# First attention weights loaded behind the last rwkv projections instead of at the end of the rwkv stage

## The chip, the cores and the metric

The kernel runs on one core of one Trainium2 chip. The metric is the device time of one execution in microseconds. The core has five engines with a program each: TensorE (PE; its weight loads are shown apart as PEld), VectorE (DVE), ScalarE (ACT), GpSimd (POOL) and SyncE (SP). They share SBUF and PSUM and wait for each other with semaphores. Here SyncE only issues DMAs, which 16 DMA engines carry out. The engines' own instructions come by the same 16 DMA engines, in packets of 16 KB, which the profile lists as the queues q8 and q14 "instruction".

## The reference

One inference step of one decoder layer, for a prompt of 1024 rows and 64 sample rows (1088 rows in all), width 1024, float32. What matters here is the first half of the layer:

```python
u = _rmsnorm(h, norm_mix)
proj = u @ w_in
P = proj[..., :RWKV_PROJ]                 # r, k, v and three small parts
q, k, v = ...                             # the other columns, 3 x 512
rw_out, new_shift, new_wkv = _rwkv7(P, shift_state, wkv_state, ...)   # 8 heads x 64
att = _rmsnorm(attend(q, k, v), attn_out_norm)                        # 8 heads x 64
h = h + jnp.concatenate([rw_out, att], axis=-1) @ w_out
```

`new_shift` is the last projected row of the prompt and of each sample, and is an output. Then follow a mixture of experts, a gated embedding and a last norm, which the change doesn't touch.

## The kernel before

The program is a row of stages: token projection inputs, small inputs, rwkv, attention, output projection, routing, experts, finish. Each stage is one block; all engines meet in a barrier at its end. Between two blocks lies a small one in which GpSimd clears the semaphores of the next (`clear`, L2292), with barriers of its own. No engine starts in the attention block before SyncE has left the rwkv block.

**rwkv** (`rwkv`, L220 ff.) works on J = 4 pairs of heads, 128 columns each. All four pairs use the same tile `g.w3`, 128 partitions x 3072 floats, with one third each for the weights of r, k and v. It outlives the stage, and attention uses the same bytes for the weights of its q, k and v (1536 KB, 12 KB in each partition). The profile calls it `w`.

TensorE's program alternates `between(j)` and `inverse_and_steps(j)`. In `between(j)` the projections of pair j+1 are cut up among the work of pair j (L415). `inverse_and_steps(j)` first does the last third of v's projection of pair j, then interleaves two things: the inverses of the chunks of pair j (L620, L622, L624: small 64x64 matmuls, in runs of up to 32) and the 17 state steps of pair j-1 (L633 to L663), each of which waits for the one before through VectorE (L1080, L1084) and ScalarE (L850). For j = 0 there are no steps, for j = 4 no inverses. I call the stretch for j = 1, 2 and 3 from its first L633 to its last step **mixed stretch** 1, 2 and 3.

SyncE's program is written by hand. For each pair it waits until a projection has been evacuated, and issues in `last_rows(q, j)` two small stores of the last rows (L350: 128 rows of 4 bytes; L351: 128 rows of 32 bytes), and behind them the load of the next pair's third of `w3` (L333, 512 KB; none for the last pair). `last_rows("v", j)` comes just as mixed stretch j begins, so a 512 KB load runs beside mixed stretches 1 and 2, and none beside 3. Behind it `load_small` (L336, L338) issues four small loads beside stretch 1, none beside 2 and 3. SyncE then waits for the state (L369, semaphore `c_sev`, set by the last step) and, much later, for the stage's result (L378). At the end of its loop it issues the load of the first attention weights (L389, semaphore `qkv_in`), then waits for all the stores (L390 to L393) and goes into the barrier.

**Attention** begins on TensorE with `project(0)`: it waits for `qkv_in` (L1221), then multiplies (L1227). SyncE begins with eight loads of tables (L1184, L1185) and the first 5 MB of the key cache (L1186). GpSimd begins with two memsets (L1211, L1213).

Of the kernel before, what the change touches and what calls it, by code (L numbers as in the profile page):

```python
# [17 lines left out]
J = H // 2  # L18
# [200 lines left out]
def rwkv(nc, g):  # L219

    with ExitStack() as ctx:
# [7 lines left out]
        k, kk, r, v, tmp = (sb(n, [128, T]) for n in ("k", "kk", "r", "v", "tmp"))  # L229
# [88 lines left out]
        s = {n: sem(n) for n in names}  # L318
# [10 lines left out]
        with nc.Block() as block:  # L329
            @block.sync  # L330
            def _(sp):
                def load_w3(q, j):
                    sp.dma_start(w3[:, KIND[q], :, :], g.d_wrkv[j, KIND[q]]).then_inc(s["w3_" + q], 16)  # L333

                def load_small(j):
                    sp.dma_start(wwa[j % 2][:, :], g.d_w2a2[:, 128 * j:128 * j + 128]).then_inc(small[j % 2], 16)  # L336
                    for i in range(3):
                        sp.dma_start(edge[j % 2][:, i, :], g.d_shT[128 * j + RW * i:128 * j + RW * i + 128, :]).then_inc(small[j % 2], 16)  # L338

                def load_wg(j):  # L340
                    sp.dma_start(wg2[j % 2][:, :], g.d_g2[:, 128 * j:128 * j + 128]).then_inc(wg_in[j % 2], 16)

                def load_s0(j):
                    sp.dma_start(s0[j % 2][:, :, :].rearrange("p b v -> p (b v)"), g.d_stT[128 * j:128 * j + 128, :]).then_inc(s0_in[j % 2], 16)

                def last_rows(q, j):
                    row = 128 * j + RW * KIND[q]
                    sp.wait_ge(s[q + "_ev"], 3 * j + 3)
                    sp.wait_ge(s[q + "_ends"], j + 1)
                    sp.dma_start(g.o_pshift[row:row + 128, :], RAW[q][:, S:S + 1]).then_inc(s[q + "_outs"], 16)  # L350
                    sp.dma_start(g.o_sshift[row:row + 128, :], ends[j % 2][:, KIND[q], :]).then_inc(s[q + "_outs"], 16)  # L351
                    if j + 1 < J:
                        sp.wait_ge(s[q + "_mm"], 3 * j + 3)
                        load_w3(q, j + 1)

                load_small(0)
                load_w3("k", 0)
                load_w3("r", 0)
                load_w3("v", 0)
                load_s0(0)  # L360
                load_small(1)
                load_s0(1)
                load_wg(0)
                load_wg(1)
                for j in range(-1, J + 1):
                    jn, jp = after(j), before(j)
                    if jp is not None:
                        sp.wait_ge(s["c_sev"], (NC + 1) * (jp + 1))
                        sp.dma_start(g.o_pwkv[128 * jp:128 * jp + 128, :], st[:, NC % 2, :]).then_inc(s["c_outs"], 16)  # L369
                        sp.wait_ge(s["d_in"], jp + 1)  # L370
                        sp.dma_start(g.o_swkv[128 * jp:128 * jp + 128, :], sn[:, :, :].rearrange("p b v -> p (b v)")).then_inc(s["c_outs"], 16)
                        if jp + 2 < J:
                            load_s0(jp + 2)
                    if jn is not None:
                        last_rows("k", jn)
                    if jp is not None:
                        sp.wait_ge(s["g_ev"], 3 * jp + 3)
                        sp.dma_start(g.rw[128 * jp:128 * jp + 128, :], cen).then_inc(s["rw_out"], 16)  # L378
                        if jp + 2 < J:
                            load_wg(jp + 2)  # L380
                    if jn is not None:
                        last_rows("r", jn)
                        last_rows("v", jn)
                        if jn + 2 < J:
                            load_small(jn + 2)

                for q in "rkv":
                    sp.wait_ge(s[q + "_mm"], 3 * J)
                sp.dma_start(g.w3[:, :], g.d_wqkv[0].rearrange("p k i c -> p (k i c)")).then_inc(g.qkv_in, 16)  # L389
                for q in "rkv":  # L390
                    sp.wait_ge(s[q + "_outs"], 32 * J)
                sp.wait_ge(s["c_outs"], 32 * J)
                sp.wait_ge(s["rw_out"], 16 * J)  # L393
# [1982 lines left out]
```

## Time and profile before

| | |
|---|---|
| median of 3 runs | 1954.55 us |
| lowest and highest | 1946.48 and 1960.20 us |
| the profiled execution | 1968.97 us |
| its span, first to last instruction | 1967.0 us |
| outside the span | 1.97 us |
| TensorE busy | 1672.5 us, 85% of the span |
| mean granted TensorE clock | 0.899 |
| rwkv stage in this execution | about 103 to 738 us |
| attention stage | about 741 to 1158 us |

The profile is one execution. It took 14.4 us (0.7%) more than the median of the runs, which differ among themselves by 13.7 us. Times in it are from the start of the span. Queue rows (SPq) show when SyncE issued a DMA and for how long it was busy issuing it; "landing" is the time from issue until the data are there. A PE row's bracket is the idle time before it and what ended it.

### The profile page before, as it was taken

What the parts mean: (1) busy time and instruction counts of PE and PEld (TensorE: products, weight loads), DVE (VectorE), ACT (ScalarE), POOL (GpSimd) and SP (SyncE); (2) the same over time, 40 slices, a digit from 0 to 9 for tenths busy, and PEclk for the clock granted to TensorE, in tenths of its full rate; (3) what the DMA queues carried; (4) which work ended last, traced back from release to release, by engine and by line L of the source; (5) the groups of instructions that cost most, each with busy time, mean ns of one, the idle gap of its engine ahead of it and who ended that gap; (6) DMA issues with size and microseconds to landing.
All of it is one profiled execution on the core that took longest, in us unless ns stands there. A gap on an engine that the chain in (4) does not pass through costs nothing. (4 is left out here: it accounts for less than half of the span.)

```text
span 1967.0 us, 34999 instructions
## 1 busy us (share of the span) xinstructions
PE 1672.5 (85%) x15260; PEld 1173.9 (60%) x15260; DVE 657.9 (33%) x1559; ACT 430.0 (22%) x856; POOL 70.3 (4%) x76
## 2 busy tenths in 40 slices
PE   3687997998998888898989889966599999990897
PEld 2355666576577666575766654452488888870443
DVE  3125455445455231514251532235011111114333
ACT  2131321321321210413132320022011111112233
POOL 0000000000000000000000000003100000004000
PEclk8888898898898658899999989988699999995899
DMA  3033031221000004424242530044399999956211
GB/s 119 12 58 24 5 21 15 34 15 21 16 2 9 13 21 188 162 108 162 108 162 108 222 132 0 0 165 193 128 357 364 362 374 364 370 205 214 108 43 38
DMA packets 61774, 247.01 MB, mean 126 GB/s; under 512 B 13745, under 2 KB 21169, under 8 KB 51889
## 3 DMA queue, kind: packets, MB, share of 16 engines
q1 hardware_dynamic: 49232, 201.70, 30.8%
q0 software_dynamic: 7776, 26.23, 3.6%
q10 hardware_dynamic: 4608, 16.78, 2.1%
q8 instruction: 123, 2.02, 0.5%
q14 instruction: 35, 0.28, 0.0%
HBM read 210.65 MB, written 34.04 MB: 124 GB/s over the span
## 5 line engine op out<-in xcount | busy, mean ns | idle before, releaser
L415 PE MATMUL bank<-h,w 128*128 128x352 f32 (+1 forms) x576 | 200.7, 499 | 6.4 <-DVE xb L978 6.4
L415 PEld LDWEIGHTS bank<-h,w 128*128 128x128 f32 x576 | 110.5, 199 | 70.6 <-issue 8.7
L2026 DVE COPY xgT<-bank 128x512 f32<-128x512 f32 x64 | 41.2, 686 | 319.2 <-PE bank L1958 319.2
L1972 PEld LDWEIGHTS bank<-xgT,we_g 128*128 128x128 f32 x1024 | 122.0, 196 | 17.7 <-issue 14.3
L1227 PE MATMUL bank<-h,w 128*128 128x352 f32 (+1 forms) x384 | 120.7, 477 | 9.7 <-DMA w<-in_wqkv 9.7
L1972 PE MATMUL bank<-xgT,we_g 128*128 128x128 f32 x1024 | 122.5, 279 | 2.8 <-DVE xgT L2026 2.8
L1972 PE MATMUL bank<-xgT,we_u 128*128 128x128 f32 x1024 | 119.6, 275 | 0.0
L1972 PEld LDWEIGHTS bank<-xgT,we_u 128*128 128x128 f32 x1024 | 116.9, 192 | 0.0
L1982 PE MATMUL bank<-we_d,hT 128*128 128x512 f32 x256 | 115.0, 592 | 0.0
L2169 PE MATMUL bank<-wp,unT 128*128 128x512 f32 x256 | 113.3, 601 | 0.0
L1227 PEld LDWEIGHTS bank<-h,w 128*128 128x128 f32 x384 | 74.1, 194 | 54.6 <-POOL qd L1213 10.3
L2169 PEld LDWEIGHTS bank<-wp,unT 128*128 128x128 f32 x256 | 48.9, 193 | 58.8 <-issue 58.8
L1982 PEld LDWEIGHTS bank<-we_d,hT 128*128 128x128 f32 x256 | 46.3, 191 | 46.4 <-issue 46.4
L1283 PE MATMUL bank<-ident,score 128*128 128x128 f32 x288 | 46.3, 295 | 27.2 <-ACT score L1402 14.1
L1243 PEld LDWEIGHTS bank<-w,h 128*128 128x128 f32 (+1 forms) x576 | 65.3, 186 | 2.6
L1958 PE MATMUL bank<-ident,xg 128*128 128x128 f32 x256 | 34.7, 280 | 37.4 <-DMA xg<-xn_rows,idx 37.4
L1243 PE MATMUL bank<-w,h 128*128 128x128 f32 (+1 forms) x576 | 66.0, 275 | 0.0
L1283 PEld LDWEIGHTS bank<-ident,score 128*128 128x128 f32 x288 | 32.6, 147 | 51.4 <-ACT score L1402 27.8
L2000 ACT ACTIVATE yo<-bank 128x512 f32<-128x512 f32 x64 | 34.7, 594 | 123.7 <-PE bank L1982 123.7
L1430 DVE TENSOR_TENSOR eT<-bank,sin 128x352 f32<-128x352 f32 (+1 forms) x24 | 12.8, 535 | 142.3 <-PE bank L1235 140.8
L1466 DVE CUSTOM_DVE_ANT_0 score<-bank,count 128x512 f32<-128x512 f32 (+3 forms) x96 | 50.8, 555 | 27.5 <-PE bank L1272 27.5
L1623 PE MATMUL bank<-cache,rwT 128*128 128x512 f32 x128 | 59.4, 618 | 0.0
(399 smaller groups left out, 2579.0 us busy)
## 6 DMA issues: line engine op xcount, KB each, us to landing
we_g<-in_weg SPq DMA_DIRECT2D x32, 1024.0 KB, 7.2
we_u<-in_weu SPq DMA_DIRECT2D x32, 1024.0 KB, 9.9
we_d<-in_wed SPq DMA_DIRECT2D x32, 1024.0 KB, 12.7
cache<-in_kcj SPq DMA_DIRECT2D x4, 5120.0 KB, 16.0
cache<-in_vcj SPq DMA_DIRECT2D x4, 5120.0 KB, 15.0
y_rows<-yo ACTq DMA_DIRECT2D x32, 512.0 KB
w<-in_wrkv SPq DMA_DIRECT2D x12, 512.0 KB, 11.5
w<-in_wqkv SPq DMA_DIRECT2D x4, 1536.0 KB, 18.2
```

The costliest lines, as they stand in the source:

```text
L415: mm = pe.matmul(out[:, 0:w], w3[:, KIND[q], kd, :], g.uT[:, kd, a:a + w], start=(kd == 0), stop=(kd == KD - 1))
L1227: mm = pe.matmul(bank[QK[i][n]][:, 0:w], w3[:, k, i, :], g.uT[:, k, a:a + w], start=(k == 0), stop=(k == KD - 1))
L1243: mm = pe.matmul(bank[2 + n % 2][0:rows, 128 * (t - t0):128 * (t - t0) + 128], g.uT[:, k, 128 * t:128 * t + rows], w3[:, k, 2, :], start=( ...
L1283: mm = pe.transpose(bank[x % 2][:, 128 * (b - b0):128 * (b - b0) + 128], score[:, i % 2, hh, 128 * b:128 * b + 128], g.ident[:, :])
L1466: dve.tensor_tensor_reduce(out=score[:, i % 2, hh, 512 * b:512 * b + w], in0=bank[4 + 2 * hh + (b if i >= 4 else i % 2)][:, 0:w], in1=coun ...
L1623: pe.matmul(bank[b + i][:, :], g.rwT[:, k, 128 * t:128 * t + 128], wo[:, k, 512 * i:512 * i + 512], start=(k == 0), stop=(k == J - 1))
L1958: mm = pe.transpose(bank[k // 4][:, 128 * (k % 4):128 * (k % 4) + 128], v[:, k, :], g.ident[:, :])
L1972: mm = pe.matmul(bank[2 + e % 2][:, 128 * (2 * a + f):128 * (2 * a + f) + CAP], w[:, k, 128 * f:128 * f + 128], xT[e % 2][:, k, :], start= ...
L1982: mm = pe.matmul(bank[4 + 2 * (e % 2) + c][:, :], hT[e % 2][:, f, :], weights[e % NW][2][:, f, 512 * c:512 * c + 512], start=(f == 0), sto ...
L2000: last = act.activation(yo[:, e % 2, 512 * c:512 * c + 512], bank[4 + 2 * (e % 2) + c][:, :], ACT.Copy)
L2026: last = dve.tensor_copy(xT[e % 2][:, 4 * c:4 * c + 4, :].rearrange("p k q -> p (k q)"), bank[c][:, :])
L2169: mm = pe.matmul(bank[4 + 2 * (t % 2) + i][:, :], uT[:, t % 2, k, :], wp[:, k, 512 * i:512 * i + 512], start=(k == 0), stop=(k == KD - 1))
```

## The change

The load of the first attention weights, with its three waits, moves from behind SyncE's loop over the pairs into the loop, behind `last_rows("v", 3)`. The waits (all projections of the stage done) are the same.

```diff
                         last_rows("v", jn)
                         if jn + 2 < J:
                             load_small(jn + 2)
-
-                for q in "rkv":
-                    sp.wait_ge(s[q + "_mm"], 3 * J)
-                sp.dma_start(g.w3[:, :], g.d_wqkv[0].rearrange("p k i c -> p (k i c)")).then_inc(g.qkv_in, 16)
+                    if jn == J - 1:
+
+                        for q in "rkv":
+                            sp.wait_ge(s[q + "_mm"], 3 * J)
+                        sp.dma_start(g.w3[:, :], g.d_wqkv[0].rearrange("p k i c -> p (k i c)")).then_inc(g.qkv_in, 16)
                 for q in "rkv":
                     sp.wait_ge(s[q + "_outs"], 32 * J)
```

The lines from 389 on have a number higher by one in the changed kernel. The orders of all engines but SyncE's are as they were. On SyncE the first place is the start of mixed stretch 3 (`raw_kv` is the projected v of pair 3, `ends` its last rows, `st` the state that the steps leave):

```order
 L350 DMA out_pshift<-raw_kv 128x1 [waits v_ends,v_ev]
 L351 DMA out_sshift<-ends 128x8
+L390 DMA w<-in_wqkv 128x3072 [waits v_mm,k_mm,r_mm]
 L369 DMA out_pwkv<-st 128x64 [waits c_sev]
 L371 DMA out_swkv<-wt 128x512 [waits d_in]
```

The weight load now stands right behind the two small stores of v's last rows, and ahead of the wait for the last step of the stretch. The second place is the end of the stage on SyncE (`rw_rows` is the stage's result in device memory):

```order
 L371 DMA out_swkv<-wt 128x512 [waits d_in]
 L378 DMA rw_rows<-xb 128x1088 [waits g_ev]
-L389 DMA w<-in_wqkv 128x3072 [waits v_mm,k_mm,r_mm]
 L329 UNCONDITIONAL_BRANCH [waits c_outs,v_outs,rw_out,k_outs,r_outs]
```

Here only the last store of the result is left ahead of the end of the block. TensorE's program at the same boundary, the same in both kernels (numbers of the changed one), is:

```order
L435 MATMUL bank<-sg,wg 128x384
L329 UNCONDITIONAL_BRANCH
L1216 UNCONDITIONAL_BRANCH [waits barrier_Pool_Activation_PE_DVE_SP_release]
L1228 MATMUL bank<-h,w 128x352 [waits qkv_in,zeroed]
L1228 MATMUL bank<-h,w 128x352 x15
```

Its first attention matmul stands behind two things, the barrier and the weight load; the change moves the second only.

## Rows read from the trace of the kernel before

**Rows 1.** Waits, TensorE, 743 to 1180 us: total, times, longest.

```profile
PE bank L1227 <- DMA w<-in_wqkv: 9.7, 1, 9.7
```

**Rows 2.** Timeline at the boundary: start, duration, engine, line, instruction, idle before.

```profile
734.94 0.33 SPq L378 DMA_DIRECT2D rw_rows<-xb  x1
735.37 0.37 SPq L389 DMA_DIRECT2D w<-in_wqkv  x1
741.36 0.20 POOL L1211 MEMSET vt<- 64x128 f32 x1 [740.90 <-POOLq L2297]
...
743.02 2.68 PE L1227 MATMUL bank<-h,w 128*128 128x352 f32 x4 [9.69 <-DMA w<-in_wqkv]
```

**Rows 3.** Waits, SyncE's queue, 640 to 760 us.

```profile
SPq L2297 <- PEq L2297: 2.9, 1, 2.9
SPq L393 <- DMA rw_rows<-xb: 2.1, 1, 2.1
```

**Rows 4.** Timeline at the next boundary, attention to output projection.

```profile
1158.51 0.95 POOL L1552 MEMSET h<- 64x1024 f32 x1 [416.52 <-POOLq L2297]
...
1158.56 3.85 PE L1600 MATMUL bank<-ones,sqsum 128*128 128x1 f32 x18 [3.93 <-PEq L2297]
```

**Rows 5.** Windows: busy PE, PEld, DVE, ACT, POOL; granted clock; DMA share; GB/s.

```profile
594.00:596.00 2.00, 2.00 (x36) 1.80 (x33) 0.95 (x4) 0.00 (x0) 0.00 (x0) 0.50 0.07 8
...
598.00:600.00 2.00, 2.00 (x89) 1.86 (x86) 1.55 (x5) 0.22 (x1) 0.00 (x0) 0.90 0.00 0
...
748.00:749.00 1.00, 1.00 (x4) 0.64 (x3) 0.00 (x0) 0.00 (x0) 0.00 (x0) 0.70 0.97 356
```

**Rows 6.** Timeline: first matmul and end of mixed stretches 1, 2, 3, and loads.

```profile
290.00 0.33 PE L633 MATMUL bank<-bv,xa 64*64 64x64 f32 x4 [1.32 <-ACT raw_kv L719]
...
337.43 0.34 SPq L369 DMA_DIRECT2D out_pwkv<-st  x1
...
438.50 0.33 PE L633 MATMUL bank<-bv,xa 64*64 64x64 f32 x4 [1.32 <-ACT raw_kv L719]
...
483.58 0.33 SPq L369 DMA_DIRECT2D out_pwkv<-st  x1
...
585.34 0.33 PE L633 MATMUL bank<-bv,xa 64*64 64x64 f32 x4 [1.32 <-ACT raw_kv L719]
...
585.81 0.43 SPq L351 DMA_DIRECT2D out_sshift<-ends  x1
...
629.52 0.33 SPq L369 DMA_DIRECT2D out_pwkv<-st  x1
```

**Rows 7.** Waits of TensorE for "issue": 120-200, 280-360, 438.5-484 and 585.3-630.5 us.

```profile
PE bank L620 <- issue: 9.0, 1, 9.0
...
PE bank L663 <- issue: 6.3, 1, 6.3
...
PE bank L622 <- issue: 6.1, 5, 4.2
...
PE bank L644 <- issue: 2.4, 1, 2.4
```

**Rows 8.** DMA issues of 438-442, 660-672 and 735-745 us: KB, us to landing.

```profile
w<-in_wrkv SPq DMA_DIRECT2D x1, 512.0 KB, 11.1
...
rw_rows<-xb SPq DMA_DIRECT2D x1, 544.0 KB, 2.7
...
w<-in_wqkv SPq DMA_DIRECT2D x1, 1536.0 KB, 7.5
...
rw_rows<-xb SPq DMA_DIRECT2D x1, 544.0 KB, 3.0
```

**Rows 9.** Instruction queue, quarter-microseconds from 587.75, 439.75, 449.25: packets, MB, share.

```profile
q8 instruction: 1, 0.02, 91.3%
...
q8 instruction: 1, 0.02, 75.3%
...
q8 instruction: 1, 0.02, 22.0%
```

## The prediction

> **What bounds the kernel now.** The change can act at two places only, where the load leaves and where it arrives, so I read the trace there and nowhere else in depth. TensorE is busy for 85% of the span and nearly always the engine that others wait for; what counts is where it stands still.
>
> I read the waits of TensorE in the attention stage first. In 437 us there is one wait for a DMA, and it is the one for the first weights: 9.7 us [rows 1]. Taken alone this line would promise 9.7 us. The timeline around it says otherwise. The load is issued at 735.37, the first matmul starts at 743.02 [rows 2], which agrees with the landing 7.5 us after issue [rows 8]. But GpSimd starts its attention program only at 741.36 [rows 2]: until then the barrier holds all. SyncE waits 2.1 us for the store of the result and then 2.9 us in the barrier and the clearing block [rows 3]. At the next boundary, where TensorE needs no DMA, it starts 0.05 us after GpSimd [rows 4]. So without the load TensorE would have started at about 741.41. Of the 9.7 us only the last 1.6 belong to the load.
>
> Then I read the place to which the load moves, the start of mixed stretch 3, with the stretches before it as comparison, since they contain the same work and stand at the same place behind the same two small stores. What the reader is to see there is a wait that is put down to "issue": TensorE stops in the middle of the small matmuls with nothing to wait for that a semaphore shows. In stretch 3, without a load, it stops once, for 2.4 us; in stretch 2, beside the 512 KB load, for 6.1 us in five pieces, the longest 4.2; in stretch 1, with small loads besides, once for 6.3; in the first run of inverses, without steps, once for 9.0 [rows 7]. The instruction queue says what it is. In stretch 3 one packet of instructions, begun at about 587.75, holds its DMA engine for 91.3% x 16 x 0.25 = 3.65 us; one of stretch 2 takes 3.0 us; one at 449.25, when the traffic has gone, 0.9 us [rows 9]. TensorE runs out of instructions while their transfer is slow, and after such a stop the granted clock is at 0.50 for some microseconds too (half of full speed, 1.2 instead of 2.4 GHz; back between 598 and 600) [rows 5]. That is a cost of the new place that the boundary's row doesn't show.
>
> **The change, part by part.**
>
> 1. *The wait at the start of attention goes.* 743.02 - 741.41 = 1.6 us off the path: TensorE is what all of attention waits for, and everything behind is chained to it. What is late next is the barrier itself, at 741.36.
>
> 2. *The barrier may come a little sooner.* The last store of the result (L378) no longer shares the DMA engines with the 1536 KB behind it. It landed after 3.0 us here, and that of the pair before, with nothing beside it, after 2.7 [rows 8]; SyncE waited 2.1 us for it at L393 [rows 3]. That is 0.3 us, at most the 2.1. I take 0.3. Sum of both: 1.9 us gained.
>
> 3. *The clock at the start of attention.* It is at 0.50 there and reaches full speed at about 748.3, 5.3 us after the first matmul [rows 5]. If this recovery follows the first matmul it moves with it and costs nothing. If it came at fixed times instead, 1.6 us more of work would run at half speed, and 0.8 of the 1.9 us were lost. I take 0 and keep 0.8 for the range.
>
> 4. *SyncE's issue moves.* 0.37 us of issuing [rows 2] go from behind L378 to behind L351, at about 585.81 + 0.43 = 586.2 [rows 6]. The three waits are for projections that were evacuated before, so they end at once. Queued behind it on SyncE is L369, which waits until 629.52 anyway [rows 6]: 43 us of cover. The load would have to take that long to be in the way of the state's store. Nothing.
>
> 5. *The load now runs beside mixed stretch 3.* Its own time isn't the question: it has 155 us to land. The question is what it does to the instruction packets. From below: a row with load against one without. Stretch 2 lasts from 438.50 to 483.58, 45.08 us; stretch 3 from 585.34 to 629.52, 44.18 us [rows 6]. The load of 512 KB thus costs 0.9 us net, although its stops are 3.7 us longer (6.1 - 2.4, [rows 7]): most comes back, since part of the time at half clock falls into the stop and the chain of steps has slack against the inverses. Stretch 1, with four small loads behind its 512 KB, lasts 290.00 to 337.43, 47.43 us, which is 3.25 us above stretch 3. The new load is three times as large as theirs. It is 128 rows of 12 KB where they are 128 rows of 4 KB. The load in stretch 2 took 11.1 us to land, though the large one, in other company, took 7.5 [rows 8]: what slows it is not its size but the two small stores ahead of it. If the damage goes by that time, it stays at 0.9; if it goes by bytes, it is 0.9 x 3 = 2.7 us. If the stop grows to the longest seen, 9.0 us, and none of it comes back, it is 9.0 - 2.4 = 6.6 us. A gain from the load isn't to be had here. I take the middle of 0.9 and 2.7, which is 1.8 us, and keep 0 and 6.6 for the range. Behind the stretch nothing absorbs it: the stage runs on as one chain to L378.
>
> Sum: -1.6 - 0.3 + 1.8 = -0.1 us on 1968.97 us of the profiled execution, that is nothing. Set against the median, 14.4 us lower for reasons that lie outside these two places, 1954.5 us.
>
> One rule of the Trainium skill speaks against term 5. Row first: one packet of instructions took 3.65 us and TensorE stood for 2.4 us [rows 7, 9]. The Trainium skill, "Runtime: NRT & Kernel Launch", section "Instruction fetch mechanics", says that the next 16 KiB block is fetched while the current one runs, so that crossing a boundary is mostly hidden. By that rule term 5 is 0 and the sum is the first rival's; in these stretches the trace doesn't agree with "hidden". 
>
> **Rivals.**
>
> *A: the gain alone, 1952.6 us.* The new load doesn't lengthen the stop in stretch 3: instruction packets are already late from the two stores alone (3.65 us for one packet without any load), and 2.4 us may be all. For it speaks that the damage of 512 KB was only 0.9 us net. Against it, that all three stretches with a load had stops of 6 us and more. 1954.55 - 1.9 = 1952.6.
>
> *B: slower, the starved TensorE.* The place is the runs of inverses from 586 to about 600. Up to 1536 KB go out ahead of the next instruction packets. From an extra cost of 1.9 us in stretch 3 on the change loses; at 6.6 us the time is 1954.55 - 1.9 + 6.6 = 1959.3 us. For it speaks that stretch 1, with more queued behind the stores, was 3.25 us longer. Against it, that the same bytes per engine flow in 4 us once nothing blocks them (7.5 us to land with the store ahead, rows 8).
>
> *C: the edit doesn't do what it says.* SyncE might not come to the new place in time, or the load might wait. The second store of v's last rows is issued at 585.81 in the trace of before [rows 6], and the load stands directly behind. I give this nothing.
>
> **How the numbers follow.** Forecast (cost between 1 and 3 us, 1953.6 to 1955.7): 0.45. A: 0.27. B with 3 to 6.6 us: 0.22. Something else, such as the clock taking another course over a longer part of the kernel: 0.06. All the named cases lie within 5 us of the median before, and 1% of it is 19.5 us, about what a measurement of this kernel can tell from no change. Only the last case can leave that band: faster by over 1% 0.03, slower by over 1% 0.04, within 1% 0.93. The range holds the cases and what runs of one kernel differ by: single runs lie 8.1 us below and 5.7 above their median, a median of a few perhaps two thirds as far. Low: 1952.6 - 6 = 1946.5. High: 1959.3 + 3.7 = 1963.
>
> **What the profile of the changed kernel would show.** Step 1: the wait of the first L1228 for the load is gone from the list and its idle time is about 7.8 us, ended by the barrier; TensorE starts within 0.1 us of GpSimd's first memset. Step 2: L378 to that memset, 6.4 us here (741.36 - 734.94), becomes 6.1. Step 3: the clock is back 5 to 5.5 us after the first L1228. Step 5: the time from the first L633 of stretch 3 to L369, 44.18 us here, becomes 45 to 47; 44.2 is rival A, over 47.5 is rival B; the "issue" wait there is 4 to 8 us instead of 2.4. The forecast is wrong if that stretch grows by more than 6.6 us, if a second long stop appears behind 600, or if work far from both places changes its clock.

## The result: slower by 0.3%

| | before | changed |
|---|---|---|
| median of 20 runs | 1953.41 us | 1958.52 us |
| lowest, highest | 1946.48, 1960.20 us | 1953.30, 1966.05 us |
| profiled execution | 1968.97 us | 1966.05 us |

The ratio is 1.0029 with a 95% interval of 1.0016 to 1.0043: 5.1 us longer by the medians. A second set of 12 runs gave 1.0017 (0.9997 to 1.0037), about 3 us longer. Forecast was no change; the time lies in the range, the direction was rival B's. The one profile of each kernel shows the opposite order, which is a lesson of its own (below).

The timeline of SyncE's queue and TensorE in the changed kernel, beside [rows 2, 6]. Here the load is issued within mixed stretch 3, and that stretch ends at 637.15 instead of 629.52:

```profile
585.39 0.33 PE L634 MATMUL bank<-bv,xa 64*64 64x64 f32 x4 [1.32 <-ACT raw_kv L720]
586.40 0.36 SPq L390 DMA_DIRECT2D w<-in_wqkv  x1
594.31 0.80 PE L623 MATMUL bank<-lw,xb 64*64 64x64 f32 x18 [4.81 <-issue]
600.75 1.22 PE L625 MATMUL bank<-xb,lw 64*64 64x64 f32 x17 [3.69 <-issue]
637.15 0.33 SPq L369 DMA_DIRECT2D out_pwkv<-st  x1
...
734.59 0.33 SPq L378 DMA_DIRECT2D rw_rows<-xb  x1
740.70 0.20 POOL L1212 MEMSET vt<- 64x128 f32 x1 [740.24 <-POOLq L2298]
741.01 0.31 POOL L1214 MEMSET qd<- 128x256 f32 x1
741.38 31.41 PE L1228 MATMUL bank<-h,w 128*128 128x352 f32 x96 [8.20 <-POOL qd L1214]
```

The stretch lasts 637.15 - 585.39 = 51.76 us, against 44.18 [rows 6]. TensorE stops twice, 4.8 and 3.7 us, with nothing to wait for that the profile shows ("issue"), where it stopped once for 2.4 [rows 7]. At the boundary the idle time before the first attention matmul is 8.2 us instead of 9.7 [rows 1], and no longer ends with the load.

The DMA view of the changed kernel from 585 to 598 us shows what the instruction queue does meanwhile. First come the busy tenths of the DMA engines and the GB/s in 40 slices, then queues and issues:

```profile
DMA  0000220990900000099900900700094004428979
GB/s 0 0 0 0 2 12 0 378 189 0 38 0 0 0 0 0 0 265 38 38 0 0 38 0 0 38 0 0 0 76 38 0 0 113 189 113 378 416 340 529
...
q1 hardware_dynamic: 373, 1.05, 83.2%
...
w<-in_wqkv SPq DMA_DIRECT2D x1, 1536.0 KB, 14.3
```

No line of an instruction queue stands there: in 13 us not one packet of instructions began. The same view of the kernel before has two of them and no load:

```profile
q8 instruction: 2, 0.03, 2.8%
q1 hardware_dynamic: 288, 0.00, 1.2%
```

Of the two stops only the second is shown to be hunger for instructions. The next lines are the packet that ends the gap, from the DMA view of 598.25 to 598.50 us, then the windows from the first matmul of the stretch to the second stop, in the changed kernel and in the kernel with the load alone beside the stretch (`e_nostore`, below), and the stop in the latter:

```profile
q8 instruction: 1, 0.02, 22.6%
...
585.39:597.06 11.67, 6.69 (x207) 5.81 (x207) 4.45 (x16) 0.65 (x3) 0.00 (x0) 0.77 0.85 56
...
565.46:570.75 5.29, 5.22 (x207) 4.70 (x207) 4.52 (x16) 0.65 (x3) 0.00 (x0) 1.00 0.81 291
...
572.72 0.50 PE L630 MATMUL bank<-xb,lw 64*64 64x64 f32 x9 [1.98 <-issue]
```

The packet begins at about 598.3 and takes 22.6% x 16 x 0.25 = 0.9 us, and TensorE goes on 1.5 us behind it. In both kernels the stop comes behind exactly 207 matmuls, a fixed place of the program. So it is in all eight profiles in which the load runs beside the stretch: a stop of 2.0 to 5.7 us behind the 207th matmul, ended 1.4 to 1.6 us after a packet of instructions. The first stop is another matter. It begins 4.1 us into the stretch, behind 157 matmuls, and ends at 594.31, when no packet has begun since 579; the early stops of `after_again`, `e_third` and `e_rows4k` end ahead of the first packet too. In the three profiles with the stores alone beside the stretch the one long stop begins after 4.1 to 4.8 us, behind 158 to 186 matmuls; where the load or the 32-byte store comes first it is missing. It goes with the stores, and what TensorE lacks there isn't shown.

The load took 14.3 us to land instead of 7.5 [rows 8]. It doesn't stream: most slices are at 0 or 38 GB/s, and only the last few at the 340 and more that it reaches otherwise. The windows of the changed kernel (columns as in rows 5) add the price in clock:

```profile
590.00:592.00 2.00, 0.00 (x0) 0.00 (x0) 0.00 (x0) 0.00 (x0) 0.00 (x0) 0.91 1.59 55
592.00:594.00 2.00, 0.00 (x0) 0.00 (x0) 0.00 (x0) 0.00 (x0) 0.00 (x0) 0.50 0.26 12
...
598.00:600.00 2.00, 0.00 (x0) 0.00 (x0) 0.00 (x0) 0.00 (x0) 0.00 (x0) 0.50 0.67 272
...
602.00:604.00 2.00, 2.00 (x36) 1.88 (x38) 0.88 (x2) 0.00 (x0) 0.00 (x0) 0.50 0.00 0
604.00:606.00 2.00, 2.00 (x66) 1.93 (x62) 0.89 (x3) 0.22 (x1) 0.00 (x0) 0.68 0.00 0
```

At half clock (602 to 604) TensorE does 36 matmuls in 2 us; at a clock of 0.90 [rows 5] it does 89. The granted clock is back at about 605 instead of 599.

**Where the two profiles mislead.** The changed kernel's profile is 2.9 us shorter than that of before. Stretch 4, the last 17 state steps and what leads up to them (from one L369 to the next), takes 77.94 us in it and 85.02 in the profile of before, where the clock stayed at half from 670 us on. The windows of the changed kernel there:

```profile
690.00:700.00 10.00, 8.36 (x170) 6.58 (x168) 2.72 (x11) 2.17 (x9) 0.00 (x0) 0.97 0.02 3
700.00:710.00 10.00, 8.94 (x168) 6.62 (x167) 3.51 (x14) 2.12 (x8) 0.00 (x0) 1.00 0.01 2
```

and the same two windows of before:

```profile
690.00:700.00 10.00, 10.00 (x142) 8.52 (x144) 2.73 (x12) 1.30 (x6) 0.00 (x0) 0.50 0.01 2
700.00:710.00 10.00, 10.00 (x144) 8.56 (x140) 2.93 (x12) 1.83 (x7) 0.00 (x0) 0.50 0.01 2
```

Either that belongs to the change, which then gives back in stretch 4 what it loses in 3, or it was an accident of one execution. That is theory 2 against theory 1 below.

### The profile page after: what moved, and what is told of

It is laid out like the page before. It is cut to its first block and busy times, and to the rows that moved or that the text cites. A ratio compares the mean times of both kernels' runs of the same rounds, so it can differ in the third digit from the quotient of the medians.

```text
span 1964.0 us, 34999 instructions
## 1 busy us (share of the span) xinstructions
PE 1661.6 (85%) x15260; PEld 1163.3 (59%) x15260; DVE 657.8 (33%) x1559; ACT 430.0 (22%) x856; POOL 70.5 (4%) x76
## 5 line engine op out<-in xcount | busy, mean ns | idle before, releaser
L1983 PEld LDWEIGHTS bank<-we_d,hT 128*128 128x128 f32 x256 | 46.3, 191 | 46.4 <-issue 46.4
```

The source lines that it names most:

```text
L1983: mm = pe.matmul(bank[4 + 2 * (e % 2) + c][:, :], hT[e % 2][:, f, :], weights[e % NW][2][:, f, 512 * c:512 * c + 512], start=(f == 0), sto ...
```

## The experiments

In the code cuts "..." stands for what is left out. Theory 1: the load behind the two small stores delays the packets of instructions, TensorE is starved in mixed stretch 3, and this costs more than the boundary gives. Theory 2: the stretch's loss is made good later, and the 5 us come from somewhere behind the boundary. Each run has a ratio to the kernel before on the same chip with its 95% interval, and one profile, from which the stretches are read as in rows 6. How far a single profile can be trusted is shown by stretch 2, which nothing touches in ten of the fourteen: it lasted 44.0 to 45.1 us in eight of them, 46.2 and 48.0 in two.

**The load behind the stretch** (`e_quiet`).

```diff
+                        if jp == J - 2:            # behind L369
+                            for q in "rkv":
+                                sp.wait_ge(s[q + "_mm"], 3 * J)
+                            sp.dma_start(g.w3[:, :], ...)
-                    if jn == J - 1:
-                        ... sp.dma_start(g.w3[:, :], ...)
```

> The load of the first attention weights is issued behind L369 of pair 2, when mixed stretch 3 is over, instead of at its start; all else as in the changed kernel. Theory 1 (TensorE starved of instructions beside the load): mixed stretch 3 is back at 44 to 45 us, the gain at the boundary (1.3 us in the profile of the changed kernel) stays, time 1951 to 1953 us, ratio to the kernel before 0.998 to 1.000. Theory 2 (the stretch's loss is made good later, as in the one profile, and the 5 us come from the earlier start of attention): attention starts just as early, so the time stays at about 1958 us, ratio 1.003.

Measured: 0.9987 (0.9959 to 1.0015). Stretch 3 is 41.87 us, and the load lands in 6.7 us. The early load without stretch 3's loss is not slower than before; theory 2's 1.003 lies outside the interval.

**The load ahead of the stores** (`e_first`); it is gone from its old place, which the cut leaves out.

```diff
                     sp.wait_ge(s[q + "_ends"], j + 1)
+                    if q == "v" and j == J - 1:
+                        ... sp.dma_start(g.w3[:, :], ...)
                     sp.dma_start(g.o_pshift[...], ...)
                     sp.dma_start(g.o_sshift[...], ...)
```

> As the changed kernel, but the weight load is issued ahead of the two small stores of v's last rows, not behind them. Theory 1 in the form that the stores clog the DMA engines and the load queued behind them dribbles (14.3 us to land in the changed kernel): the load lands in 4 to 6 us, mixed stretch 3 is 46 to 48 us instead of 51.8, ratio to before 1.000 to 1.001. Theory 1 in the form that bytes alone delay the instructions: stretch 3 stays at 50 to 53 us, ratio 1.003. Theory 2: ratio 1.003.

Measured: 0.9977 (0.9953 to 1.0001). The same load at nearly the same time, 0.9 us earlier, ahead of the stores in the queue. The timeline of this kernel:

```profile
576.33 0.33 PE L633 MATMUL bank<-bv,xa 64*64 64x64 f32 x4 [1.32 <-ACT raw_kv L719]
576.43 0.34 SPq L353 DMA_DIRECT2D w<-in_wqkv  x1
576.81 0.43 SPq L354 DMA_DIRECT2D out_pshift<-raw_kv  x1
577.28 0.44 SPq L355 DMA_DIRECT2D out_sshift<-ends  x1
619.06 0.33 SPq L373 DMA_DIRECT2D out_pwkv<-st  x1
```

The stretch is 42.73 us, even less than expected, and the load lands in 7.4 us instead of 14.3 (4 to 6 were expected). Bytes alone don't do the damage.

**The load without the stores** (`e_nostore`): as in the changed kernel, with both stores of pair 3's v moved behind L369.

```diff
+                    if q != "v" or j < J - 1:
                         sp.dma_start(g.o_pshift[...], ...)
                         sp.dma_start(g.o_sshift[...], ...)
```

> As the changed kernel, but the two small stores of v's last rows of pair 3 are issued behind L369, after mixed stretch 3, so that the load runs alone beside it. Stores clog: load lands in 4 to 5 us, stretch 3 is 42 to 45 us, ratio to before 0.998 to 1.000. Bytes alone: stretch 3 stays near 50 us, ratio 1.002 to 1.003. Theory 2: 1.003.

Measured: 0.9978 (0.9960 to 0.9996). Stretch 3 is 41.73 us, landing 7.3 us, again more than the 4 to 5 expected. The instruction packets come evenly here, one every 3.5 to 5.0 us from 570.4 on, 4.95 us into the stretch; in the changed kernel the first comes 12.9 us into it. The intervals of this run and of the last two lie below the 1.0016 to 1.0043 of the changed kernel; against its second set (0.9997 to 1.0037) only this run's does.

**A third of the load** (`e_third`). TensorE's wait for `qkv_in` is raised to match the two loads.

```diff
-  sp.dma_start(g.w3[:, :], ...)
+  sp.dma_start(g.w3[:, 0:1024], ...[:, 0:1024])     # at the start of stretch 3
+  sp.dma_start(g.w3[:, 1024:3072], ...)             # behind L369
```

> As the changed kernel, but only a third of the weights (512 KB, 128 rows of 4 KB, the form of the loads beside stretches 1 and 2) is loaded at the start of mixed stretch 3, the other two thirds behind L369. Damage by bytes: a third of 7.6 us, stretch 3 about 46.5 us, ratio 1.001. Damage by the number of rows queued behind the stores: stretch 3 stays at 50 us or more, ratio 1.003. By the row of stretch 2 of the kernel before: 45 us, ratio 1.000.

Measured: 1.000 (0.998 to 1.002); stretch 3 is 46.37 us, the 512 KB land in 10.6 us. That is 2.3 us over the 44.1 of before, a third of the 7.3 of the whole, but by one profile, and less than the untouched stretch 2 differs between profiles.

**The changed kernel once more** (`after_again`), nothing edited.

> The changed kernel once more, for a second profile and for its place beside the other runs. Theory 1: mixed stretch 3 is again 49 to 53 us. The short stretch 4 (77.9 us there, 85.0 in the kernel before) was 77.5 to 80.1 in the four kernels run since, so the 85.0 was an accident of the granted clock in the one profile of before, and stretch 4 is again 77 to 80 us here; ratio 1.002 to 1.004. Theory 2 (what stretch 3 loses is made good in stretch 4): stretch 4 is longer wherever stretch 3 is shorter, which those four already speak against.

Measured: 1.0017 (0.9997 to 1.0037). Stretch 3 is 50.97 us, with stops of 5.7 and 2.4; stretch 4 is 79.17.

**Rows of 4 KB** (`e_rows4k`): three DMAs of 1024 columns instead of one of 3072, with TensorE's wait raised to match.

```diff
-  sp.dma_start(g.w3[:, :], ...)
+  for i in range(3):
+      sp.dma_start(g.w3[:, 1024 * i:1024 * i + 1024], ...)
```

> As the changed kernel, but the 1536 KB are loaded by three DMAs of 128 rows of 4 KB instead of one of 128 rows of 12 KB, at the same place behind the stores. If the damage goes by bytes behind the stores, mixed stretch 3 stays at 50 to 53 us, ratio 1.003. If long rows are what hurts (each instruction packet behind a 12 KB row), it falls to 46 to 48 us, ratio 1.000 to 1.001.

Measured: 1.0015 (0.9992 to 1.0038); stretch 3 is 47.89 us, between the whole (51.8, 51.0) and the third (46.4). This one profile would give the length of the rows about half of the damage, but 3 to 4 us is what an untouched stretch can differ by, and the run times can't tell this kernel from the changed one. That the length of rows matters isn't shown.

**All loads ahead of their stores** (`e_allfirst`).

```diff
                     sp.wait_ge(s[q + "_ends"], j + 1)
+                    if j + 1 < J:
+                        ... load_w3(q, j + 1)
+                    elif q == "v":
+                        ... sp.dma_start(g.w3[:, :], ...)
                     sp.dma_start(g.o_pshift[...], ...)
                     sp.dma_start(g.o_sshift[...], ...)
```

> In every call of last_rows the weight load goes ahead of the two small stores, for all pairs and for r, k and v, and the first attention weights ahead of v's last stores. Theory 1 as it stands now (neither stores nor load alone hurts, a load queued behind the stores does): mixed stretches 1, 2 and 3 are about 42 to 43 us each (47, 45 and 44 in the kernel before) and the long stop in the first inverses, 9.0 us, shrinks to 2 to 3; time 1936 to 1942 us, ratio 0.992 to 0.995. If it holds only for the large load, ratio 0.998 as with the load alone ahead.

Measured: 0.9918 (0.9886 to 0.9950). The mixed stretches are 41.22, 40.87 and 43.02 us, and the stop in the first inverses, 9.0 us in [rows 7] and 5.9 to 9.0 in the six profiles read with the old order there, is 2.6. Against the kernel before this is 0.8%; against `e_first` (0.9977), which has the early load ahead too, the order of the other loads is worth some 0.6%.

**All of v's traffic behind the stretches** (`e_behind`).

```diff
                         sp.dma_start(g.o_pwkv[...], ...)        # L369
+                    if 0 <= j < J:
+                        if jp is None:
+                            sp.wait_ge(s["w_ev"], 4)
+                        last_rows("v", j)
+                        if j + 2 < J:
+                            load_small(j + 2)
+                        if j == J - 1:
+                            ... sp.dma_start(g.w3[:, :], ...)
```

> For every pair the last rows of v, the next v weights, the small loads, and for the last pair the first attention weights are issued behind the mixed stretch (behind L369, for pair 0 when the first small projection of pair 1 is out), so that no traffic of SyncE's queue runs beside any mixed stretch. Theory 1: the three mixed stretches are 41 to 43 us, the stop of 9 us is gone; ratio 0.991 to 0.994. The rival: ScalarE waits for v's stores before it writes the next k (the tile is shared), and a store issued later makes it wait; then the time between the stretches grows by up to 9 us each and the ratio is 1.000 or above.

Measured: 0.9834 (0.9809 to 0.9860), more than expected. Against the profile of `before_again`, stretch 1 begins 7.0 us earlier and the three stretches are 16.0 us shorter together, 23 us of the 23.1 between the two profiled executions. The stretches are 40.09, 38.61 and 39.63 us; between them lie 101.41 and 101.70 us against 101.07 and 101.76 before, so ScalarE loses nothing by the later stores. In stretch 3 TensorE has no "issue" wait longer than 0.6 us:

```profile
PE bank L628 <- issue: 0.7, 2, 0.5
...
PE bank L637 <- issue: 0.6, 1, 0.6
```

The load stands behind the stores here too, and lands in 13.0 us. It does no harm: from L369 to L378 it is 35.38 us, and 35.35 in `e_behind_end`, where the load isn't there. There are no long runs of 64x64 matmuls beside it; that this is the reason is argued, not shown.

**The kernel before once more** (`before_again`), nothing edited.

> The kernel before once more, for a second profile. If the 85.0 us of stretch 4 was an accident, it is 77 to 80 us here; mixed stretch 3, with the two stores and no load beside it as in the kernel with the load behind L369, is 41.5 to 44.5 us. The ratio to itself is 1.

Measured: 0.9990 (0.9966 to 1.0015). Stretch 3 is 43.97 us and stretch 4 77.89. In the windows of stretch 4 the clock is at full speed, as in the changed kernel:

```profile
680.00:690.00 10.00, 8.89 (x170) 6.60 (x166) 3.50 (x14) 2.12 (x8) 0.00 (x0) 1.00 0.01 3
690.00:700.00 10.00, 7.69 (x144) 5.76 (x144) 4.08 (x14) 2.01 (x8) 0.00 (x0) 1.00 0.02 5
```

**One store ahead of the load** (`e_one_store`): the store of 128 rows of 4 bytes goes behind L369, that of 32 bytes stays ahead of the load.

```diff
+                    if q != "v" or j < J - 1:
                         sp.dma_start(g.o_pshift[...], ...)
```

> As the changed kernel, but of the two small stores of v's last rows only the one of 128 rows of 32 bytes stays ahead of the load; that of 128 rows of 4 bytes is issued behind L369. If the number of small rows ahead of the load sets the damage, stretch 3 falls half of the way, to 46 to 47 us, ratio 1.000 to 1.001. If the 4-byte rows are the culprit it is 42 to 43 us, ratio 0.998; if the 32-byte rows, it stays at 50 us or more, ratio 1.002.

Measured: 0.9992 (0.9969 to 1.0014). Stretch 3 is 40.99 us and the load lands in 7.3 us: 128 rows of 32 bytes ahead of it do nothing.

**The same deferral, attention's load at the end** (`e_behind_end`): `e_behind` with the load of the first attention weights back at the old place, the end of the stage.

> As the kernel with all of v's rows, loads and small loads behind the mixed stretches, but the first attention weights are loaded at the end of the stage as in the kernel before. It tells what the early load is worth where it harms nothing: by the profiles 1.3 to 1.7 us at the boundary, so ratio 0.984 to 0.985 against 0.9834; L378 to the first attention matmul is 8.1 us again instead of 6.8.

Measured: 0.9847 (0.9823 to 0.9870) against 0.9834 for `e_behind`; the intervals overlap, so run times don't resolve what the early load is worth. The profile does: L378 to the first attention matmul is 8.04 us, against 6.79 in `e_behind`.

**Both remedies** (`e_behind_first`): `e_behind` with each weight load ahead of its stores.

> The kernel with everything of v's behind the mixed stretches, and besides the weight load ahead of the two small stores in every call. If what is left of the stops near the other loads is small (the runs of small matmuls lie only in the mixed stretches), it gains nothing more: ratio 0.983 to 0.984. If the loads of k and r behind their stores still cost 1 to 2 us each, ratio 0.979 to 0.981.

Measured: 0.9803 (0.9780 to 0.9826), median 1915.57 us. It is the fastest of all; its interval overlaps that of `e_behind`, so the last 0.3% aren't shown.

Together, stretch 3 in one profile of each kernel:

| beside mixed stretch 3 | stretch 3, us | load lands, us | "issue" waits, us | early stop, stop behind 207 matmuls, us |
|---|---|---|---|---|
| nothing (`e_behind`, `e_behind_end`, `e_behind_first`) | 39.6, 38.5, 39.1 | | 2.1, 1.1, 1.5 | neither |
| small stores alone (before, `before_again`, `e_quiet`) | 44.2, 44.0, 41.9 | | 3.6, 4.4, 3.0 | early 2.4, 2.9, 2.2 |
| load alone (`e_nostore`) | 41.7 | 7.3 | 3.1 | 207: 2.0 |
| load, then stores (`e_first`, `e_allfirst`) | 42.7, 43.0 | 7.4, 7.6 | 4.7, 4.0 | 207: 2.1, 2.4 |
| 32-byte store, then load (`e_one_store`) | 41.0 | 7.3 | 3.5 | 207: 2.7 |
| stores, then 512 KB (`e_third`) | 46.4 | 10.6 | 5.8 | 2.5 and 3.3 |
| stores, then 3 x 512 KB (`e_rows4k`) | 47.9 | 11.5 (median of 3) | 7.4 | 2.7 and 3.3 |
| stores, then 1536 KB (changed, `after_again`) | 51.8, 51.0 | 14.3, 14.6 | 10.3, 9.5 | 4.8 and 3.7, 2.4 and 5.7 |

The two stops have a condition each: the early one needs the stores ahead, the 4-byte one among them; the other needs the load beside the stretch. With the stores ahead of the load there are both, and the second is longer than with the load alone.

## Why the prediction was wrong

**The step that failed is term 5**, "I take the middle of 0.9 and 2.7, which is 1.8 us". It measured 51.76 - 44.18 = 7.6 us, and 50.97 - 43.97 = 7.0 in the second pair of profiles, above even the upper end of 6.6. Rival B had the place and the sign, and was priced a little low; its starved TensorE is shown for the later of the two stops. The working of term 5 went wrong at four points.

- *The comparison row was not one.* The 0.9 us came from stretch 2, with 512 KB, against stretch 3, with stores alone. It took the two stretches for equal. With nothing beside them they last 38.6 and 39.6 us (`e_behind`), 37.5 and 38.5 (`e_behind_end`), 37.4 and 39.1 (`e_behind_first`), so stretch 2 is 1.0 to 1.7 us shorter by itself. In stretch 3 itself the 512 KB cost 46.37 - 44.1 = 2.3 us, by one profile.
- *The stop was discounted.* The same paragraph had stops 3.7 us longer in stretch 2 and let most of it come back. It set all the "issue" waits of stretch 2, 6.1 us, against the longest alone of stretch 3, 2.4; all of stretch 3's are 3.6, so the difference was 2.5. In the changed kernel the "issue" waits grew from 3.6 to 10.3 us in stretch 3, 6.7 us, and the stretch by 7.6; in the second pair from 4.4 to 9.5, and by 7.0. Nothing came back; the half clock after the stops fits what is on top.
- *The 2.4 us weren't of the kind the load adds.* They were read as hunger for instructions, and that stop was then lengthened. The load adds a stop of its own behind the 207th matmul, 3.7 and 5.7 us, for which packets of instructions are late; whether the early stop is the same hunger isn't shown.
- *"What slows it is not its size" was half right.* The 4-byte store ahead, alone or with the other, is what makes the load slow: landing 7.3 us without it, 14.3 behind it. Given the stores, size seems to count: landing 10.6 us for 512 KB and 14.3 for 1536, 2.3 and 7.3 us of damage, with one profile of the smaller load.

**Steps 1 and 2**, the boundary: forecast 1.6 + 0.3 = 1.9 us from L378 to the first matmul. Measured 8.08 - 6.79 = 1.3 us, and the same 6.77 to 6.80 in each kernel with the early load. Step 2 was right (6.42 us from L378 to GpSimd's first memset became 6.11). Step 1 was 1.0 instead of 1.6: I had said that the barrier is late next and read the start from the next boundary, but TensorE's wait names `zeroed` besides `qkv_in`, and GpSimd ends its second memset at 741.01 + 0.31 = 741.32. The order of TensorE's program had shown that. The first matmul came 0.68 us after GpSimd's first memset, not within 0.1.

**Step 3**, the clock there: rows 5 (0.70 of full speed over 748 to 749) put the return of the full clock at 748.6, not at 748.3. From the first matmul to ScalarE's first copy it takes 7.3 to 7.8 us in the three profiles with the load at the end, and with the early load either 6.6 to 6.9 (seven profiles) or 7.9 to 8.0 (four). The recovery neither follows the first matmul exactly nor costs the 0.8 us that I kept for it regularly; with it, the boundary's gain is between 0.5 and 2.5 us.

**Step 4** held: SyncE issued the load at 586.40, and L369 was waiting for the steps, not for SyncE. In sum the profiles give 7.3 - 1.3 = 6.0 us net, against 5.1 and about 3 us measured in the two sets of runs.

**Rival A** fell, as a load behind the 4-byte store does add to the stops. The sentence that carried it, that an instruction packet is slow from the two stores alone, was true (3.65 us), and the stores alone cost 2.3 to 5.7 us more than nothing at all beside the stretch (41.9 to 44.2 against 38.5 to 39.6). Theory 2 fell with `before_again`: 77.9 us in stretch 4 with a stretch 3 of 44.0.

The rule of the Trainium skill, "Runtime: NRT & Kernel Launch", "Instruction fetch mechanics", that the fetch is mostly hidden holds in these stretches only when the queue is quiet ("issue" waits of 2.1 us in `e_behind`). The other, "DMA: Bandwidth & Descriptors", "Queues, rings and completion order", that a completion comes behind all earlier writes of its DMA engine, agrees with a fetch that is late behind the load; it was not tried by itself.

**What stays open.** What TensorE lacks in the early stop. Why 128 rows of 4 bytes hold up what stands behind them, while 128 rows of 32 bytes don't; whether it is the row's length or the source (one column of a large tile) wasn't tried. Nor was the 4-byte store alone ahead of the load, so that both together are needed isn't excluded. The stores don't fill the DMA engines: the 288 packets of the view of before take 1.2% x 16 x 13 = 2.5 us in all. What begins just behind them is slow: in the changed kernel 16 rows of the load begin between 587 and 588.5 and take 4.8 us each on average, none begins in the next 2 us, and those at 598.3 take 0.46. What holds them isn't shown. Stretch 3 with stores alone was 44.2, 44.0 and 41.9 us in three profiles, and I can't say what makes that 2 us.

## What to carry to other kernels

A load that is moved off a barrier goes beside something. Ask what the engines there are fed by, their own instructions included: here a run of short matmuls was a bad place for DMA traffic, above all for a large load queued behind stores of a few bytes. Try the load ahead of the tiny stores, or both when the engine is in longer instructions; here that was worth 0.8% and 1.7%, and both 2.0%, the early load included, where removing the visible 9.7 us wait had about 1.3 us to give (0.5 to 2.5 with the clock's course). Don't price an edit by one profile of each side: a stretch that the edit doesn't touch differed by 7 us through the clock alone.

## What was not expected of the hardware

- Order in one queue decides. The same 1536 KB and the same two stores within 0.9 us: 7.4 us to land with the load first, 14.3 with it last. In `e_behind` the slow landing, 13.0 us, cost nothing.
- Instruction packets can stay away for 13 us: in the changed kernel none began from 585 to 598 us. TensorE stood twice in that time and just behind it, 8.5 us in all; the second stop is theirs.
- Stretch 4 with its 17 state steps ran from its second half on at half clock in one of fourteen profiles and took 85.0 us; in the others it took 77.1 to 80.2.
